# Second mixer's output projection: the recurrent half as three rounded products, with weight low parts made on GpSimd

## The reference

```
y = concat([rms(attn, out_gain[:512]), rms(rec, out_gain[512:])])   # 256 x 1024
x = x + gate * (y @ w_out)                                          # w_out: 1024 x 1024
h = rms(x, norm_gain[l, 1]) * (1 + scale) + shift
# layer 1: router logits of h, top 2 of 8, then the chosen experts' SwiGLU
```

## Time and profile before

| | |
|---|---|
| median of 3 runs | 1435.79 us (1435.27 to 1437.94) |
| profiled execution | 1435.91 us |
| its span | 1434.2 us, so 1.7 us lie around it |
| PE busy | 1398.1 us, 97% of the span |
| DVE, ACT, POOL busy | 1237.1, 898.7, 45.2 us |
| chain that ended last | PE 87%, DVE 6%, DMA 3%, ACT 2% |
| HBM traffic | 483.9 MB, 337 GB/s over the span |

### The profile page before, as it was taken

The page is one execution under the profiler, slowest core; times in us unless marked ns, Lnnn a source line. Parts: engine busy times, 40 slices in busy tenths (PEclk is TensorE's granted clock), DMA queues, the critical chain, the costliest instruction groups (busy, mean ns, idle before and its releaser), DMA issues.

```text
span 1434.2 us, 18304 instructions
## 1 busy us (share of the span) xinstructions
PE 1398.1 (97%) x6878; PEld 1137.2 (79%) x6878; DVE 1237.1 (86%) x1088; ACT 898.7 (63%) x792; POOL 45.2 (3%) x79
## 2 busy tenths in 40 slices
PE   5989999999999999999999999999999999999999
PEld 2765899996875888888888888888888888888886
DVE  3689768776878899999999999899999999999997
ACT  2074534443274677777777777777777777777774
POOL 0000000000000000000000000000000000000012
PEclk9999999999999999999999999999999999999999
DMA  9966669868627899999999999999999999999995
GB/s 368 414 255 217 241 221 372 296 258 337 241 109 278 298 364 375 358 394 396 340 395 395 340 398 394 391 346 393 395 340 396 396 341 397 393 382 356 393 391 149
DMA packets 195824, 484.50 MB, mean 338 GB/s; under 512 B 8926, under 2 KB 31684, under 8 KB 191684
## 3 DMA queue, kind: packets, MB, share of 16 engines
q1 hardware_dynamic: 187056, 451.17, 83.9%
q0 software_dynamic: 6480, 32.52, 6.1%
q10 hardware_dynamic: 2244, 0.22, 0.1%
HBM read 473.40 MB, written 10.49 MB: 337 GB/s over the span
## 4 chain that ended last, share of the span: by engine, by line
PE 87%; DVE 6%; DMA 3%; ACT 2%; SPq 1%; issue 1%; DVEq 0%; ACTq 0%
PE ps L1053 21%; PE ps L1055 21%; PE ps L1054 21%; PE ps L713 3%; PE ps L903 2%; PE ps L904 2%; PE ps L905 2%; PE ps L869 2%; PE ps L1096 2%; DMA split<-in_w_in 2%; PE ps L706 1%; SPq L456 1%; PE ps L911 1%; DMA arena<-in_w_ada 1%; PE ps L913 1%; PE ps L912 1%
## 5 line engine op out<-in xcount | busy, mean ns | idle before, releaser
L1970 DVE TENSOR_TENSOR split_r<-arena,split_r 128x2048 fp32r<-128x2048 f32 x336 | 763.6, 2289 | 62.0 <-ACT split_r L1379 61.5
L1379 ACT ACTIVATE split_r<-arena 128x2048 fp32r<-128x2048 f32 x334 | 640.4, 1918 | 125.2 <-PE ps L1055 121.9
L1053 PE MATMUL ps<-split_r,tokens_r 128*128 128x512 f32 x1280 | 505.4, 395 | 0.0
L1055 PE MATMUL ps<-split_r,tokens_r 128*128 128x512 f32 x1280 | 499.3, 390 | 0.0
L1054 PE MATMUL ps<-split_r,tokens_r 128*128 128x512 f32 x1280 | 498.3, 389 | 0.0
L1055 PEld LDWEIGHTS ps<-split_r,tokens_r 128*128 128x128 f32 x1280 | 240.3, 188 | 51.1
L1054 PEld LDWEIGHTS ps<-split_r,tokens_r 128*128 128x128 f32 x1280 | 240.7, 188 | 48.1
L1053 PEld LDWEIGHTS ps<-split_r,tokens_r 128*128 128x128 f32 x1280 | 240.5, 188 | 47.8 <-DVE split_r L1970 0.4
L903 PE MATMUL ps<-tokens_r,split_r 128*128 128x256 f32 x352 | 98.9, 281 | 1.3 <-DVE hT_r L1818 1.0
L904 PE MATMUL ps<-hT_r,split_r 128*128 128x256 f32 x352 | 99.3, 282 | 0.0
L905 PE MATMUL ps<-tokens_r,split_r 128*128 128x256 f32 x352 | 98.6, 280 | 0.0
(11 more groups left out here) (355 smaller groups left out, 1314.6 us busy)
## 6 DMA issues: line engine op xcount, KB each, us to landing
arena<-in_moe_w_gate SPq DMA_DIRECT2D x57, 2048.0 KB, 10.6
arena<-in_moe_w_up SPq DMA_DIRECT2D x57, 2048.0 KB, 10.9
arena<-in_moe_w_down SPq DMA_DIRECT2D x56, 2048.0 KB, 10.3
arena<-in_w_ada SPq DMA_DIRECT2D x15, 1024.0 KB, 20.1
arena<-in_w_ada POOLq DMA_DIRECT2D x10, 1536.0 KB, 10.3
arena<-in_ffn_w_gate SPq DMA_DIRECT2D x11, 1024.0 KB, 5.6
arena<-in_ffn_w_up SPq DMA_DIRECT2D x11, 1024.0 KB, 13.2
arena<-in_ffn_w_down SPq DMA_DIRECT2D x11, 1024.0 KB, 14.9
```

Of the source, the lines that this page charges most:

```text
L1053: mm(out_, xh, h, start=first, stop=False, skip_group_check=True)
L1055: return mm(out_, xl, h, start=False, stop=last_, skip_group_check=True)
L1379: A(wh[:, j % SPLITS, :], piece_half(j), ACT.Copy).then_inc(sem("w_hi"), 1)
L1970: v.tensor_tensor(wl[:, j % SPLITS, :], piece_half(j), wh[:, j % SPLITS, :].bitcast(F32), ALU.subtract).then_inc(sem("w_lo"), 1)
```

## The change

Layer 1's recurrent half of the output projection becomes three rounded products per block. ACT makes the rounded copy of the four weight blocks (`out_high`) into slot 1 of `arena`, three of them ahead of `turned_q(1, 6)` and one after the gelu's tanh. POOL makes their low parts in place (`out_low`). ACT writes the recurrence's output rounded into `hTr`, and DVE makes its low part (`low_rec`) after the first `update`. Since slot 1 now holds `out_hi` up to the end of the projection, piece 1 moves to the end of the first seven and waits for `wout_done` 16. Two things leave DVE for POOL: the addition of the gate's bias, and the low part of half 0.

```
+        y_lo = part(tokensr, D, LT, SEQ)
+        out_hi = part(arenar, PIECE, LT, D)
...
-        for i in range(SLOTS):
-            fills.append(("moe", 0, i, None, {0: [("rec_ps", 4)], 2: [("rec", 2)], 3: [("rg_ps", 4)], 5: [("wout_done", 13)]}.get(i, [])))
+        OUT_HI = 1
+        for i in [i for i in range(SLOTS) if i != OUT_HI] + [OUT_HI]:
+            fills.append(("moe", 0, i, None, {0: [("rec_ps", 4)], OUT_HI: [("wout_done", 16)], 2: [("rec", 2)],
+                                              3: [("rg_ps", 4)], 5: [("wout_done", 13)]}.get(i, [])))
@@ POOL
+            def out_low(i):
+                pool.wait_ge(sem("f_hi"), UNITS + i + 1)
+                g.tensor_tensor(out_rows(LT + i, splitr), out_rows(LT + i, split), out_hi[:, i, :].bitcast(F32),
+                                ALU.subtract).then_inc(sem("f_lo"), 1)
+            for i in range(LT - 1):
+                out_low(i)
             pool.wait_ge(sem("ada_red"), 4)
             g.dma_start(moe_gate_bias, b_ada[1, 1, 2 * D:].unsqueeze(0)).then_inc(sem("late_bias_in"), 16)
+            out_low(LT - 1)
+            pool.wait_ge(sem("late_bias_in"), 32)
+            g.tensor_tensor(moe_gate_acc[0:1, :], moe_gate_acc[0:1, :], moe_gate_bias, ALU.add)\
+                .then_inc(sem("gate_ok"), 1)
+            pool.wait_ge(sem("w_hi"), 1)
+            g.tensor_tensor(wl[:, 0, :], piece_half(0), wh[:, 0, :].bitcast(F32), ALU.subtract)\
+                .then_inc(sem("w_lo"), 1)
@@ PE
+                def project_split(t, half, bank):
+                    cols = slice(half * 512, (half + 1) * 512)
+                    for i in range(LT):
+                        yh, yl = (src[:, t * P:(t + 1) * P] for src in (hTr[:, LT + i, :], y_lo[:, i, :]))
+                        h, lo = out_hi[:, i, cols], out_rows(LT + i, splitr)[:, cols]
+                        mm(ps[:, bank, :], yh, h, start=(i == 0), stop=False, skip_group_check=True)
+                        mm(ps[:, bank, :], yh, lo, start=False, stop=False, skip_group_check=True)
+                        last = mm(ps[:, bank, :], yl, h, start=False, stop=(i == LT - 1), skip_group_check=True)
+                    last.then_inc(sem("wout_done"), 1)
...
+                if l == 1:
+                    pe.wait_ge(sem("f_lo"), UNITS + LT)
+                    pe.wait_ge(sem("mT_d"), DEPTH + 1)
@@ ACT
+                def out_high(i):
+                    wait_fill(act, "wout", 1, (LT + i) // 3)
+                    A(out_hi[:, i, :], out_rows(LT + i, split), ACT.Copy).then_inc(sem("f_hi"), 1)
+                if l == 1:
+                    for i in range(LT - 1):
+                        out_high(i)
                 turned_q(1, 6)
...
                 A(lq, lq, ACT.Tanh, scale=GELU_B).then_inc(sem("g_tanh"), 1)
+                if l == 1:
+                    out_high(LT - 1)
...
-                    last = A(mT[:, LT + i, :], lx[:, i, :], ACT.Copy,
+                    last = A((mT, hTr)[l][:, LT + i, :], lx[:, i, :], ACT.Copy,
@@ DVE, called after update(0, 0, 0) in layer 1
+                def low_rec():
+                    dve.wait_ge(sem("mT_a"), 4)
+                    for i in range(LT):
+                        last = v.scalar_tensor_tensor(out=y_lo[:, i, :], in0=lx[:, i, :],
+                                                      scalar=colA[:, OG + 8 + LT + i:OG + 9 + LT + i],
+                                                      in1=hTr[:, LT + i, :].bitcast(F32), op0=ALU.mult,
+                                                      op1=ALU.subtract)
+                    last.then_inc(sem("mT_d"), 1)
...
-                if l == 1:
-                    dve.wait_ge(sem("late_bias_in"), 32)
-                    v.tensor_tensor(moe_gate_acc[0:1, :], moe_gate_acc[0:1, :], moe_gate_bias, ALU.add)\
-                        .then_inc(sem("gate_ok"), 1)
...
-                if l == 1:
-                    low(0, 0)
-                else:
+                if l == 0:
...
+                dve.wait_ge(sem("w_lo"), 1)
                 low(0, 1)
```

More of the change, by code:

```diff
@@ L103, in trunk @@
         HALFP = PIECE // 2
-        arena = sb("arena", SLOTS * PIECE)
+        arena, arenar = two_views("arena", SLOTS * PIECE)
         CELL = 3 * D
@@ L352, in ada_cols, with out_rows @@
             return 2 * D if a < 2 else 3 * D
+        def out_rows(k, view):
+            at = (landed["wout", 1, k // 3][0] - SPLIT0) * CELL + (k % 3) * D
+            return view[:, at:at + D]
+        UNITS = len(units)
         ffn_gate_bias = place(0, CELL)[0:1, 2 * D:]
@@ L889, in mixer @@
                             pe.wait_ge(sem("ms"), rec_ms[l])
-                        project(t, half, LT, 2 * t + half)
+                        if l == 0:
+                            project(t, half, LT, 2 * t + half)
+                        else:
+                            project_split(t, half, 2 * t + half)
             def dense():
@@ L1780, in mixer @@
                         update(t, half, 0, rs[:, t:t + 1])
+                        if (l, t, half) == (1, 0, 0):
+                            low_rec()
                     if l == 0:
                         steps("ada", 1, (6 + t,))
-                if l == 1:
-                    dve.wait_ge(sem("late_bias_in"), 32)
-                    v.tensor_tensor(moe_gate_acc[0:1, :], moe_gate_acc[0:1, :], moe_gate_bias, ALU.add)\
-                        .then_inc(sem("gate_ok"), 1)
                 dve.wait_ge(sem("rss_ps"), l + 1)
```

## The result

| | before | after |
|---|---|---|
| median | 1436.79 us (4 runs, 1435.27 to 1437.94) | 1451.11 us (4 runs, 1449.32 to 1451.70) |
| profiled execution | 1435.91 us | 1449.32 us |
| its span | 1434.2 us | 1447.6 us |

The changed kernel is slower by 14.3 us, a ratio of 1.0099 [1.0087, 1.0111]. The direction was predicted, the size was not: 1446.6 us, with a range up to 1450.0, lies under the measured median. From profile to profile it is 13.4 us. The other 0.9 is which executions were profiled: that of after lies 1.8 us under its median (it is the fastest of its four), that of before 0.9 us under its own.

A forecast was written before the change was run, and what follows sets the result against it. PE's uninterrupted expert matmuls bound the kernel, so the start of `gather(0)` sets the end: 7.6 (moved piece) + 1.0 (POOL beside DVE) + 2.2 (clock) = +10.8 us on 1435.8, giving 1446.6 us; range 1442.8 to 1450.0.

The forecast's parts named there:

- The moved piece: Piece 1, read last, lands after piece 6 at 474.9 us; the gather starts at 478.8 us: +7.6 us.
- About 12 us: ACT's idle time ahead of the high part of half 2, waiting for piece 1.
- PE's products: 48 products in 10.9 us replace the recurrent projection's 13.8 us; the 2.9 us gain is lost in the wait.
- ACT's copies: Four copies over 128x1024, 1.04 us each, three in 3.17 us of idle time ahead of `turned_q(1, 6)`: no cost.
- `low_rec`: Four DVE operations, 1.66 us, between first and second `update`, covered by PE's groups: no cost.
- The clock: PE's clock falls while it stands ahead of the gather, which then runs slower: +2.2 us, between 0 and 3.8.
- POOL beside DVE: POOL's fourth subtraction disturbs DVE's recurrence at L1749 and delays `rec`: +1.0 us, between 0 and 2.9.
- rival A: Where POOL and DVE read wide tensors, one stands for the other's whole operation: +12.4 us, 1448.2 us; chance 0.27.
- Half 0's low part: POOL's subtraction, at most 5.7 us, starts near 449 us, ends by 455, needed past 460: covered.
- B: The clock doesn't fall in PE's stand ahead of the gather: +8.6 us, 1444.4 us; chance 0.13.
- D: Piece 1 shares engines with pieces 5 and 6, lands near 468 to 471 us, clock holds: 0 to +3 us; chance 0.10.
- C: Piece 1 is there when ACT comes to it, PE's 2.9 us reach the end: 1432.9 us; chance 0.05.

The follow-up runs named there:

- the idle products: Changed kernel plus nine 128x512 matmuls, results unused, while PE stands ahead of the gather: 1449.19 us, ratio 1.0087 to the kernel before.
- the order alone: Changed kernel with piece 1 read behind piece 4, ahead of pieces 5 and 6, instead of last: 1440.36 us, ratio 1.0035 to the kernel before.

## Why the prediction was off, point by point

**The moved piece: right, in place, mechanism and size.** The whole of it was in the queue. 7.6 us predicted, 7.7 us in the account, 7.95 us when it was the only edit; ACT stood 9.1 us for the DMA, and PE's own gain of 2.9 us vanished in that wait. "About 12 us" for ACT's stand was too long because ACT came to it later than predicted, behind `rec` and a held `update`.

**PE's products, ACT's copies and `low_rec`: right.** 10.96 us for the 48 products (10.9 predicted), three copies in 2.94 us ahead of `turned_q(1, 6)`, which then waited for 0.3 us (the 3.17 us of cover in the earlier trace rows was just enough), `low_rec` in 1.67 us.

**The clock: right, in size too.** 2.2 us in the trace, 2.1 by the idle products, 2.3 with the move alone. That it fits to a tenth is luck: 2.2 was a choice between 0 and 3.8, and gathers at the lower clock took 5.43 to 6.36 us in the traces here, 1.6 to 2.6 more than 3.81. It fell at other places as well: in the kernel after also in the attention projection (15.67 us against 13.97 where it stayed up), behind a stand of 2.00 us, and behind one of 1.40 us ahead of the norm's turn (0.50 in the window of 464 us). There it cost nothing, since the piece's wait came later; with the piece out of the way it could cost something.

**POOL beside DVE: this is the step that failed.** "I take 1.0, between them and nearer nothing, since most meetings fall where DVE has slack." The bounds were 0 and 2.9 us, and it measured 4.0. Three things were wrong in it.
- The mechanism was rival A's: DVE stands until POOL's whole operation ends. It was given 0.27.
- The meetings were counted too low. The upper bound had only the fourth subtraction in it. The bias addition stood in the text as an operation that nobody asks for before 456 us, which was true, and nobody was asked whom *it* holds: L1800, 1.24 us. And the cover for the first three was ACT's; DVE's own row maxima stood behind `taps` in its queue, and through them 1.05 us reached the attention (ACT's idle 1.02 us at 415.07, released by DVE's `mx`). 1.05 + (3.04 - 1.22) + (2.46 - 1.22) = 4.1 us; 0.1 of it was slack. Rival A had the first two, as "up to 1" and 1.7 us, though it expected the second on L1749; the third was in nobody's sum.
- Half 0's low part was "covered" by when it was needed. It too held an `update` for 2.5 us. In the kernel after the wait for piece 1 hides that. With the piece earlier it shows: from `rec` to the gather it is 31.0 us with the order alone and 29.6 us with nothing on POOL. Of these 1.4 us, 0.9 is PE's longer stand ahead of the norm's turn (1.39 us against 0.45), and about 0.5 is PE coming to it later.

With 4.0 in place of 1.0 the sum is 13.8 (13.9 with the 7.7 us measured for the piece), less the 0.5 us by which this execution began its mixer sooner: the measured 13.4. The remaining 1.9 us up to the median are the profiled execution being the fastest of four; the prediction's 1446.6 assumed it near the median in both, as that of before lay 0.1 us from the median of the three runs known then. A fourth run has since moved the median of before from 1435.79 to 1436.79 us.

The range reached 14.3 us up from 1435.8, and the change came to 14.3 us from 1436.8, at the very edge. In that upper end two errors offset each other: POOL's upper bound was 1.1 us too low, the clock's 1.6 us too high.

**The rivals.** A was nearest (1448.2). B and D fell with the clock's 0.50 and the 9.1 us of ACT. C asked for piece 1 by 467.3 us; it came at 478.5. (For the full gain C names 463 us; by its own working, a gather 2.9 us sooner less 3.9 us, it is 464.4.) C's 2.9 us exist all the same: a kernel with the same products, but with the piece earlier and POOL empty, is 2.7 to 3.3 us faster than before.

**What stays open.** Why the clock falls in one execution and not in another: up to the gather the kernel with the idle products is the kernel after, and behind a stand of 1.99 us its attention projection took 13.97 us, where after took 15.67 behind 2.00. The order alone ran in 1438.3 to 1443.2 us, wider than before's 1435.2 to 1437.7. Its profiled execution, the fastest, had a mean clock of 0.998, and the longest 0.992, but no trace of the longest is there to place the loss.

## What to carry to other kernels

When work is moved to an idle engine, list for each of its operations not only who waits for the result but who runs beside it, with the place of both one's operands; in these traces a DVE operation with two inputs in SBUF stood behind the POOL operation that was reading SBUF when it came, however small either was, and POOL stood behind DVE where DVE was first. When a tile takes over a buffer, find the transfer that used it, and ask where in its in-order queue it lands now: a 2 MB piece moved behind five others cost more than all the arithmetic that was saved. And test the idea apart from its placement: the products were worth their 2.9 us from the first.

## What the runs showed of the hardware

- POOL's subtraction took 2.36 us for 128x1024 and 4.62 us for 128x2048 (DVE 1.22 and 2.29). Its addition of 1x1024 took 3.32 us, of which the 2.19 us behind DVE's L1793 are as long as a subtraction of 128x1024 behind a DVE operation (405.21 + 2.59 - 405.57 = 2.23 us): one partition saved nothing.
- The hold strikes operations of 8 and 4 columns: 2.20 and 1.15 us in place of 0.17. Operations with one input in PSUM were not held: the reduction (1.21 us), and L1819, 0.75 us at 454.25 in the kernel after, in the midst of POOL's subtraction, while the `update` behind it stood.
- A memset on POOL didn't hold a DVE operation with two inputs in SBUF (1.22 us beside it), but a `TENSOR_SCALAR` on `mx` ended with it (0.38 us in place of 0.17).
- The clock fell behind PE stands far shorter than the 3.59 us of the earlier trace rows: behind one of 2.00 us ahead of 431.14 us after, behind one of 1.40 us ahead of 461.09 us after, and in another run in the attention, where from 408 us on no stand had been longer than 0.82 us. With a stand of 1.99 us it stayed up in the kernels with the idle products and with the bias on DVE (13.97 us each).
